# Conformer's 31-tap convolution on TensorE: four taps of 32 channels contracted at once, from copies made by DMA

## The reference, cut to what matters

```python
def causal_depthwise_conv(x, w):      # k = 31 taps, one filter for each channel
    return lax.conv_general_dilated(x, w[:, None, :], window_strides=(1,),
        padding=[(k - 1, 0)], dimension_numbers=("NWC", "WIO", "NWC"),
        feature_group_count=x.shape[-1])

def conformer_conv_mixer(x, w_pw1, b_pw1, w_dw, b_dw, ln_g, ln_b, w_pw2, b_pw2):
    h = x @ w_pw1 + b_pw1
    a, gate = jnp.split(h, 2, axis=-1)
    h = a * jax.nn.sigmoid(gate)
    h = causal_depthwise_conv(h, w_dw) + b_dw
    mean = jnp.mean(h, axis=-1, keepdims=True)
    var = jnp.mean(jnp.square(h - mean), axis=-1, keepdims=True)
    h = (h - mean) * lax.rsqrt(var + LN_EPS) * ln_g + ln_b
    return jax.nn.silu(h) @ w_pw2 + b_pw2

for i in range(4):                    # retention, conformer, short conv, retention
    x = x + rms_norm(mixer[i % 3](rms_norm(x, g[i, 0])), g[i, 1])
    x = x + rms_norm(squared_relu_mlp(rms_norm(x, g[i, 2])), g[i, 3])
```

## Time and profile before

| | us |
|---|---|
| median of 3 runs (2147.73 to 2149.37) | 2147.88 |
| the profiled execution's own time | 2145.18 |
| its span in the profile | 2143.4 |
| convolution on TensorE, 1177.6 to 1232.6 of the span | 55.0 |
| layer norm, to the first matmul of `rows_out` at 1241.6 | 9.0 |

### The profile page before, as it was taken

The page is one execution under the profiler, slowest core; times in us unless marked ns, Lnnn a source line. Parts: engine busy times, 40 slices in busy tenths (PEclk is TensorE's granted clock), DMA queues, the critical chain, the costliest instruction groups (busy, mean ns, idle before and its releaser), DMA issues.

```text
span 2143.4 us, 32132 instructions
## 1 busy us (share of the span) xinstructions
PE 2055.2 (96%) x14122; PEld 1796.5 (84%) x14122; DVE 1261.0 (59%) x1310; ACT 942.0 (44%) x1065; POOL 62.8 (3%) x87
## 2 busy tenths in 40 slices
PE   7999999999999899999999899999999999999998
PEld 5788998887989797778988479888888979777897
DVE  4765555676554565666556265556665566566554
ACT  6554344664443433344344254444344353334443
POOL 0000000000000000000000000000000000000000
PEclk9999999999999999999999999999999999999999
DMA  7233655342555465435545135555455555444552
GB/s 239 99 99 118 206 177 169 109 158 90 179 196 178 152 201 173 157 118 197 196 157 178 43 105 195 173 196 196 157 177 186 187 191 178 157 157 142 196 193 98
DMA packets 182861, 346.93 MB, mean 162 GB/s; under 512 B 14913, under 2 KB 25537, under 8 KB 182722
## 3 DMA queue, kind: packets, MB, share of 16 engines
q1 hardware_dynamic: 182722, 344.88, 48.3%
HBM read 343.81 MB, written 1.05 MB: 161 GB/s over the span
## 4 chain that ended last, share of the span: by engine, by line
PE 88%; DVE 5%; ACT 3%; DMA 2%; issue 2%; SPq 0%; POOL 0%; DVEq 0%; POOLq 0%; ACTq 0%
PE psD L1931 15%; PE psD L1932 14%; PE psD L1936 12%; PE psD L1915 11%; PE psD L1916 11%; PE psD L1920 10%; PE psD L1934 2%; DVE wl L1071 2%; PE psD L2547 2%; ACT wh L617 2%; PE psD L2209 1%; PE psD L2163 1%; DMA raw<-in_w_in 1%; DVE AL L1096 1%; PE psD L2282 1%
## 5 line engine op out<-in xcount | busy, mean ns | idle before, releaser
L1071 DVE TENSOR_TENSOR wl<-raw,wh 128x2048 fp32r<-128x2048 f32 (+2 forms) x328 | 725.5, 2220 | 486.5 <-ACT wh L617 484.5
L617 ACT ACTIVATE wh<-raw 128x2048 fp32r<-128x2048 f32 (+2 forms) x328 | 606.4, 1855 | 569.6 <-PE psD L1934 263.7
L1915 PE MATMUL psD<-AH,wh 128*128 128x256 f32 x2112 | 600.8, 284 | 8.1 <-DVE wl L1071 6.1
L1916 PE MATMUL psD<-AL,wh 128*128 128x256 f32 x2112 | 598.5, 283 | 0.0
L1920 PE MATMUL psD<-AH,wl 128*128 128x256 f32 x1976 | 560.0, 283 | 0.0
L1915 PEld LDWEIGHTS psD<-AH,wh 128*128 128x128 f32 x2112 | 406.0, 192 | 12.2 <-issue 7.3
L1916 PEld LDWEIGHTS psD<-AL,wh 128*128 128x128 f32 x2112 | 406.2, 192 | 1.8
L1920 PEld LDWEIGHTS psD<-AH,wl 128*128 128x128 f32 x1976 | 379.8, 192 | 0.0
L1931 PE MATMUL psD<-wh,HH 128*128 128x512 f32 x880 | 353.5, 402 | 13.5 <-DVE HL L1704 6.6
L1932 PE MATMUL psD<-wl,HH 128*128 128x512 f32 x880 | 350.4, 398 | 0.0
L1936 PE MATMUL psD<-wh,HL 128*128 128x512 f32 x748 | 297.5, 398 | 0.0
(11 more groups left out here) (347 smaller groups left out, 1775.5 us busy)
## 6 DMA issues: line engine op xcount, KB each, us to landing
raw<-in_mlp_w SPq DMA_DIRECT2D x128, 1024.0 KB, 5.3
raw<-in_ret_w_in SPq DMA_DIRECT2D x48, 1024.0 KB, 5.2
raw<-in_w_gate SPq DMA_DIRECT2D x20, 1024.0 KB, 5.1
raw<-in_w_up SPq DMA_DIRECT2D x20, 1024.0 KB, 5.1
raw<-in_w_down SPq DMA_DIRECT2D x20, 1024.0 KB, 5.2
raw<-in_w_in SPq DMA_DIRECT2D x16, 1024.0 KB, 7.2
raw<-in_ret_w_out SPq DMA_DIRECT2D x16, 1024.0 KB, 5.1
raw<-in_cf_w_pw SPq DMA_DIRECT2D x12, 1024.0 KB, 6.5
```

What stands on the lines that cost most here:

```text
L617: e.activation(wh[q % NHL][:, 0:kt * n], raw[q % NRAW][:, 0:kt * n], ACT.Copy).then_inc(*up("act_wh", q))
L1071: e.tensor_tensor(wl[q % NHL][:, 0:kt * n], raw[q % NRAW][:, 0:kt * n], wh[q % NHL][:, 0:kt * n].bitcast(F32), ALU.subtract).then_inc(*up( ...
L1915: e.matmul(o, hi[:, k, fs], xh, start=kk == 0 and f % 2 == 0, stop=False, skip_group_check=True)
L1916: e.matmul(o, hi[:, k, fs], xl, start=False, stop=False, skip_group_check=True)
```

## The change

Tap k = 4g + j, for g = 0 to 7 and j = 0 to 3 (tap 31 is zero). `XA`, `XB` and `XC` hold, for each 32 channels b, four copies of HP's rows: on partitions 32j to 32j+31 the 32 channels moved on by j tokens. One matmul of 128 rows by 32 columns then sums four taps, and eight of them a whole tile; the four b write four groups of 32 partitions of one bank. The copies are made by `four_taps`: 16 DMAs for each of XA (tiles 1 to 3), XB (4 and 5), XC (6 and 7), of 32 partitions by 858, 571 and 571 elements. SP issues all of XA and j = 0, 1 of the others, ScalarE j = 2, 3. `WD` holds the filter moved on by j on the same partitions, from four DMAs at Conformer's start, and `tap_squares` is now four small instructions for each tile, in Conformer. `part`, `whole` and the copies to `VT` are gone; four banks take turns, so TensorE waits for the squares of n-4. `XB` lies over `AH` and `AL`, two of the three `WT` buffers over `XS`.

```diff
+TAPS = {"a": (1, 3), "b": (4, 2), "c": (6, 2)}
...
+        def four_taps(e, x, js, signal):
+            f0, n = TAPS[x]
+            w = n * (S + 31) - 3
+            for j in js:
+                for b in range(4):
+                    e.dma_start({"a": XA, "b": XB, "c": XC}[x][32 * j:32 * j + 32, b, 0:w], HPF[32 * b:32 * b + 32, f0 * (S + 31) + j:f0 * (S + 31) + j + w]).then_inc(*landed(signal, j, b))
```

On SP, between the wait for "scaled" and the loads of `G`:

```diff
+                if kind == 1:
+                    for j in range(4):
+                        e.dma_start(WD[32 * j:32 * j + 32, :, 0:248 - j], A["vec"][:, V_DW + j:V_DW + 248].rearrange("(b c) k -> c b k", b=4)).then_inc(*landed("dma_wd", j))
```

On SP, between the load of `B2` and `load_to(first["m", i] + 2)`:

```diff
+                    load_to(first["y", i])
+                    e.wait_ge(*at("pool_set", "hp"))
+                    e.wait_ge(*at("dve_cf", "hp", 3))
+                    four_taps(e, "a", range(4), "dma_xa")
+                    load_to(first["y", i] + 2)
+                    e.wait_ge(*at("dve_cf", "hp", 5))
+                    four_taps(e, "b", (0, 1), "dma_xb0")
+                    e.wait_ge(*at("dve_cf", "hp", 7))
+                    four_taps(e, "c", (0, 1), "dma_xc0")
```

On ScalarE, in `conformer`, behind the two halves:

```diff
-                e.wait_ge(*at("dve_cf", "f0"))
-                e.activation(SS, HC[:, 0, :], ACT.Square).then_inc(*up("act_cf", "sq0"))
+                high_to(c + 2)
+                e.wait_ge(*at("dve_cf", "hp", 5))
+                e.wait_ge(*at("pool_set", "hp"))
+                four_taps(e, "b", (2, 3), "dma_xb1")
+                e.wait_ge(*at("dve_cf", "hp", 7))
+                four_taps(e, "c", (2, 3), "dma_xc1")
                 for n, f in enumerate(CONV):
...
-                    e.wait_ge(*at("pe_cf", "part", n))
-                    for a in range(2):
-                        e.activation(VT[:, 4 * (n % 2) + 2 * a:4 * (n % 2) + 2 * a + 2, :], p[a][:, :, 0:S], ACT.Copy).then_inc(*up("act_cf", "part", n, a))
...
                     e.activation(SQ[n % 2], o, ACT.Square, bias=col).then_inc(*up("act_cf", "sq", n))
+                    if n == 0:
+                        e.wait_ge(*at("dve_cf", "f0"))
+                        e.activation(SS, HC[:, 0, :], ACT.Square).then_inc(*up("act_cf", "sq0"))
```

On VectorE (`gated(b)` is the old scaling and gating of one half, L1777 to L1782; the new calls replace the loop over b):

```diff
+            def tap_squares(n):
+                f = CONV[n]
+                e.wait_ge(*at("pool_set", "wd"))
+                if n >= len(WT):
+                    e.wait_ge(*at("pe_cf", "whole", n - len(WT)))
+                for b in range(4):
+                    w = WT[n % len(WT)][:, 256 * b:256 * b + 256].rearrange("p (g m) -> p g m", g=8)
+                    e.tensor_tensor(w, bc(I4, 1, 8), bc(WD[:, b, 31 * f:31 * f + 29:4], 2, 32), ALU.mult).then_inc(*up("dve_tap", *((n,) if b == 3 else (n, b))))
...
+                low_to(c + 6)
+                c += 4
+                e.wait_ge(*at("act_norm", "rb", 2 * i + 4))
+                e.wait_ge(*at("pe_used", c - 1))
+                gated(0)
+                low_to(c + 3)
+                tap_squares(0)
+                tap_squares(1)
+                taps(8)
+                e.wait_ge(*at("pe_used", c + 1))
+                e.tensor_tensor(VT[:, 4:8, :], four(2), bc(RB, 1, 4), ALU.mult).then_inc(*up("dve_cf", "rg", 1))
+                tap_squares(2)
+                low_to(c + 4)
+                taps(12)
+                c += 4
+                e.wait_ge(*at("pe_used", c - 1))
+                gated(1)
+                low_to(c + 1)
+                tap_squares(3)
+                taps(18)
+                tap_squares(4)
                 taps(31)
+                tap_squares(5)
                 e.wait_ge(*at("dve_cf", "tap", 30))
                 e.tensor_tensor(HC[:, 0, :], HC[:, 0, :], VR, ALU.add).then_inc(*up("dve_cf", "f0"))
+                tap_squares(6)
+                low_to(c + 2)
```

On TensorE:

```diff
                 for n, f in enumerate(CONV):
+                    x = "a" if n < 3 else "b" if n < 5 else "c"
+                    tile, at_ = {"a": XA, "b": XB, "c": XC}[x], (f - TAPS[x][0]) * (S + 31)
                     e.wait_ge(*at("dve_tap", n))
...
+                    if n == 0:
+                        e.wait_ge(*at("dma_xa", 3, 3))
+                    elif n in (3, 5):
+                        e.wait_ge(*at(f"dma_x{x}0", 1, 3))
+                        e.wait_ge(*at(f"dma_x{x}1", 3, 3))
+                    if n > 3:
+                        e.wait_ge(*at("act_cf", "sq", n - 4))
+                    for g in range(8):
+                        for b in range(4):
+                            o = bank(n % 4)[32 * b:32 * b + 32, 0:S]
+                            w = WT[n % len(WT)][:, 256 * b + 32 * g:256 * b + 32 * g + 32]
+                            m = tile[:, b, at_ + 4 * g:at_ + 4 * g + S]
...
```

84 lines of the change are left out of this document (22 added, 62 removed).

## The result

The changed kernel takes **2117.81 us** (median of 4 runs, 2112.76 to 2119.3), the kernel before beside it 2147.81 (4 runs, 2145.79 to 2149.37): ratio 0.9857, 95% interval 0.9838 to 0.9875, 30 us less. Run again twice in other comparisons, it gave 2116.28 against 2145.23 (0.9864, 0.9846 to 0.9882) and 2117.72 against 2145.55 (0.9872, 0.9854 to 0.9889), so the gain is 28 to 30 us. The forecast was 2121.7 with 2119.0 to 2132.0: right in direction and in the place of the gain, 3.9 us too slow, 1.2 outside the range.

What follows compares the result with a forecast made beforehand. The convolution was taken as bound by TensorE running short of instructions. Start 1177.6, seven tiles, a 1.5 us wait and 0.3 for WD put the last set at 1206.0, 26.2 us gained: 2121.7 us, range 2119 to 2132.

Steps and rivals of the forecast that it cites:

- a set of four put at 0.24 us: TensorE, convolution: four matmuls side by side every 0.24 us, 3.84 us a tile, 26.9 us for seven; upper bound 0.36.
- the waits put at 1.5 us: Convolution, before n=5: TensorE waits 1.5 us for ScalarE's square of n=1, which stands behind VectorE's sum "f0".
- the start of the convolution put at 1177.9: End of the projection: convolution begins at 1177.6 as before, plus 0.3 us for WD's loads.
- the 2.7 us from the profiled execution to the median: Whole kernel: the median stood 2.7 us above the profiled execution; the gain was taken off the median, giving 2121.7.
- rival A: Convolution: one instruction shortage or late copies beside full DMA, 3.7 us gap then half clock; 2127.4 us, chance 0.17.
- Rival E: Convolution, before n=5: half clock at the new wait, +1.7 us, 2123.4; counted within the forecast's chance of 0.64.
- the step "1177.6 + 0.3": Projection: WD's four loads ahead of chunk s+3 cost 0 to 2.5 us, taken as 0.3, nearly covered.
- cover of 2 us: Convolution, n=3: XB's copies land at 1186.9 and are wanted at 1189.1, so the copies cost 0.
- B: Convolution: weight loads show between sets, 0.36 us a set, 2133.9 us, or 2127 if half shows; chance 0.13.
- C: Copies for the convolution run at a fraction of the rate seen, 50 GB/s: end near 1240, no gain; chance 0.04.
- D: Convolution: the four column places don't run beside each other, 15.4 us a tile, slower at 2201 us; chance 0.02.
- signs of being wrong: DMA waits at n=0, 3 or 5, convolution "issue" gaps over 1 us, sets 0.3 us or more, projection over 0.5 late.

Runs made afterwards that it cites:

- e2: Changed kernel without the copies to XB and XC, tiles 4 to 7 reading XA (values wrong): median 2116.13 us, convolution 28.05 us.
- v1b: Second run of the changed kernel with XB and XC copies on three queues and a third square buffer: median 2117.29 us, convolution 28.54 us.
- v2: Changed kernel with three copy queues, a third square buffer and WD loaded behind chunk s+5: median 2118.62 us, convolution 27.91 us.
- b2: Kernel before with 23 of 31 taps over half the tokens, same number of instructions: median 2145.86 us beside 2145.67, convolution 53.51 us.
- e4: Changed kernel with a third square buffer and ScalarE's square of tile 0 one tile later: ratio 0.9843 to 0.9892, convolution 27.69 us.
- e5: Changed kernel without XB and XC copies (values wrong) and with the third square buffer and later square: median 2114.24 us, convolution 24.77 us.
- v3: Changed kernel, two queues, third square buffer, four taps moved behind the second gating on VectorE: median 2117.54 us, convolution 25.64 us.
- b1: Kernel before with chunk loads from s+11 on held back until the fifth tile (n = 4) is whole: ratio 1.0005 to 1.0026, convolution 58.05 us.
- v1: First run of the changed kernel with XB and XC copies on three queues and a third square buffer: median 2118.10 us, convolution 25.36 us.

## Why the prediction was wrong, step by step

The mechanism held: fewer instructions, a convolution of half the length, the layer norm behind it unchanged. What failed is the size of terms of the sum. In the trace: a set of four put at 0.24 us (0.2165 measured); the waits put at 1.5 us (3.8), because the issue of a copy was put at 0.41 us (0.64 to 0.81) and ScalarE's time in it at nothing; and the start of the convolution put at 1177.9 (1176.77), since the half clock ahead of it was taken as fixed. Errors of -2.6, +2.3 and -1.1 us largely cancelled, which is luck. Behind the trace: the 2.7 us from the profiled execution to the median, taken over without scatter (-0.4 measured), 3.1 of the 3.9 us and what put the time outside the range.

By starts, in the profiled execution: forecast last set 1206.0, measured 1204.58.

- **Start of the convolution, forecast 1177.9, measured 1176.77: -1.1.** WD's loads did push the third unit back (+28.41 to +29.44, 1.0 us where I took 0.3; 0 and 1.5 in the other two profiles, all inside the bounds 0 to 2.5; in the six profiles without these early loads it starts at +28.41 to +28.46). But 1.5 us came off behind it, since the half clock of the earlier trace rows didn't come. I had read that row, used it to price rivals A and E, and taken it as fixed for the projection: the step "1177.6 + 0.3" priced the WD loads only as a delay. 0.3 of the 1.1 is the mark, which was itself earlier.
- **Sets, forecast 111 x 0.24 = 26.6, measured 111 x 0.2165 = 24.0: -2.6.** The price of a set was too high, and its bound too narrow: "a set can hardly be faster than 0.24 (0.02 of reading...)". From two sets with 0.24 between them I took the value and, for the low end, only 0.6 us, since I held the last two tiles alone to count.
- **Waits, forecast 1.5, measured 3.8: +2.3.** The wait for "f0" would have been seen (2.13 in e2) but for the others. "0.41 each" for a copy was mis-sized, 0.64 to 0.81: it was taken from the issue of a load from HBM. I had bounded it for ScalarE up to 1 us and then took 0, on the ground that ScalarE was free only at "f0" anyway. It was late for tile 0's square instead, which n=4 needs, and that chain I had not followed. XB landed by 1188.87, not 1186.9; the "cover of 2 us" was gone twice over, because n=3 wanted it at 1187.2 and not at 1189.1. Faster sets uncovered the copies.
- **VectorE.** Squares 1.42 to 1.43 for a tile's four (1.45), "f0" done at 1195.1 (1196.9), first sum begun at 1198.53 (1200.6): the order and the prices held, all of it 1.4 to 2.1 us earlier, 1.4 already at the gating of tile 5 (1180.1 for 1181.5).
- **The sum.** -1.1 - 2.6 + 2.3 = -1.4 for the last set; 0.6 came back behind it (911.77 against 911.20): the profiled execution took 2118.23 against 2119.0, 0.8 off. The other 3.1 of the 3.9 us is the step from one execution to the median. I carried the 2.7 us over, by which the median before stood above its profiled execution; after, the median stands 0.4 below. A profiled execution is one draw, and mine had no term in the range for it.
- **Right:** no gain from the MLP, layer norm as before, no "issue" gap (rival A), no weight load between sets (B), no copies at a fraction of the rate (C; XA's 1.76 MB went out in 11.5 us, 153 GB/s, and XB was late by its issue), four column places beside each other (D). Rival E happened in e2, and at n=3 instead of n=5 in v1b and v2, not in the changed kernel's three profiles.
- **Of my signs** the 448 records, the layer norm and the MLP held. Three of my signs of being wrong came: waits for DMA at n=3 and n=5, and a third unit of the projection 1.0 us late. XA, "before 1170", was issued until 1172.3; TensorE didn't wait for it, wanting it at 1176.77, but chunk s+9 behind it came late (forecast to be issued by 1166.6, it was issued from 1172.33 on), and ScalarE with it. XB, "before 1188", held n=3 until 1188.87.

## What to carry to other kernels

Where a stage has very many small instructions, halve its data and see (b2): if the time stays, it is paid per instruction, and packing more contraction into each pays until the array's time or the next wait takes over. Here a quarter of the records took half the time. When a stage gets twice as fast, list for each of its inputs when it lands against when the faster stage will want it, with the fastest price that the rows allow, not the likeliest. A small number of microseconds of "cover" is the first to go, and waits that lie side by side must be removed together (e2, e4 against e5). A profiled execution is one draw, so a forecast of the median needs a term for that in its range. A gain of 28 us stands clearly over executions that differ by 10; one of 2 us inside a stage, as in v3, can be shown by that stage's rows and not by the median.

## What the runs showed of the hardware that was not expected

- A copy from 32 partitions of SBUF to 32 others takes 0.63 to 0.84 us of SP's or ScalarE's queue with two queues, whether it moves 107, 71 or 36 KB, and up to 1.07 with three; GpSimd issued one in 0.49 to 0.53. Copies of 71 KB landed after 2.1 to 2.5 us with two queues and after 2.9 to 4.2 with three.
- TensorE's instructions come by DMA, 16 KB and some 256 at a time, and beside loads at 371 to 408 GB/s they come late: "issue" gaps of 3.3 to 3.7 us moved with the loads (b1). With a quarter of the matmuls there was none at 240 GB/s.
- TensorE's clock in a stage can turn on 0.1 us of waiting ahead of it, or on what goes with that: behind a wait of 1.80 to 1.84 us it was half in nine profiles, behind 1.47 to 1.72 us full in nine, and the projection took 24.7 us or 23.2. One program (v1, v1b) fell on either side.
